# Retention's query-state products of the sample group in 32-column strips, four batches at a time, in two groups

## The chip, the core and the metric

The kernel runs on one core of a Trainium2 chip. Five engines work side by side and meet through semaphores: TensorE (PE in the profile, with its weight loads as PEld), VectorE (DVE), ScalarE (ACT), GpSimd (POOL) and SyncE (SP). The metric is the device time of one execution in microseconds (us), taken as the median of several runs.

## What is computed

One decoder layer for a prompt of 256 tokens and for 8 sample batches of 4 new tokens (32 tokens), 288 tokens in all, with the same weights: a SwiGLU block, then retention and RWKV-7 side by side, a gated merge, and a second SwiGLU block. All numbers are float32. The change touches the sample group's retention, where each batch and head has a state S of 256 x 512 that is read by the queries and then renewed:

```python
def retention_chunk(S, q, k, v, log_g):
    ...
    scores = jnp.einsum('bihd,bjhd->bhij', q, k) * mask[None]
    inner = jnp.einsum('bhij,bjhe->bihe', scores, v)
    ...
    cross = jnp.einsum('bihd,bhde->bihe', q, S) * q_dec[None, :, :, None]
    ...
    S_new = (jnp.exp(log_g * C)[None, :, None, None] * S
             + jnp.einsum('bjhd,bjhe->bhde', k * k_dec[None, :, :, None], v))
    return S_new, inner + cross
```

## The kernel before

**Stages.** The first SwiGLU block and the projections of the first head run first. Then come four units, one for each retention head (RH = 4); a unit is one head of retention and two pairs of RWKV heads (`rw0`, `rw1`). After them the output products and the second SwiGLU block run.

**The weave.** Between the dependent steps of a unit TensorE works on products that depend on nothing in the unit: units 0 to 2 carry the projections of the next head (18 weight blocks), unit 3 the gates (32 blocks). A block is cut into 8 pieces; a piece is two weight tiles by three products (L463 to L465), six matmuls. `GAPS` is a list of named places in the unit, each with a weight, and `parts` deals the 144 pieces (256 in unit 3) over them in proportion. Every engine walks the same list with `weave(name)`: TensorE computes the pieces there; VectorE makes half of a block's low part (L1192) at every fourth piece, and waits there for ScalarE's high part (L874), which ScalarE makes at every eighth, as soon as TensorE has finished the block before; at the last piece of a block ScalarE or VectorE reads a result out of PSUM (VectorE with the rotation L1353 to L1361 at pieces 63 and 79). So a gap's weight sets how long TensorE has other work while VectorE, ScalarE and GpSimd prepare the next step, and also where their shares of the weave stand between their own steps.

**Retention in a unit, in TensorE's order.** Transposes of v and k; scores (L581 to L585); the prompt's new state, two products of 128 x 512 in banks 6 and 7 (L593); the prompt's output (L601, L603, banks 4 and 5); the samples' own part in bank 6 (L612); then for each of the 8 batches two query-state products of 32 rows x 512 columns into partitions 0 to 31 of bank 6 (L620), and two products for the batch's new state (L626) into one of three banks in turn (7, 4, 5). VectorE adds each of these to the state in place (L1427) and counts it in `s_new`; product u waits for update u-3. `q_own` holds a batch's queries and zeros for the other batches, so that the 8 batches sum in one bank. Then ScalarE copies the 32 rows to `o_s` (L1045), TensorE turns them (L548) and the norm follows (L640).

**The states' slots.** `s_ret` has four slots (SLOTS) for eight batches. ScalarE's queue sends the renewed state of a batch to memory (L1041); GpSimd's queue brings batch b+4 into its slot once that has landed (`bring`). In that queue the RWKV rows `last` and the prompt's states `s_out` go out before the second four batches come in.

**VectorE ahead of the updates.** It masks the scores (L1408), makes `k_own` (L1417), then runs `shifts`, about 40 small operations for the RWKV pairs of the same unit (L1377 to L1384), and only then begins with the updates L1427.

## Time and profile before

| | us |
|---|---|
| median of 3 runs (3253.01 to 3257.9) | 3256.34 |
| span of the profiled execution | 3245.0 |
| TensorE busy in it | 3125.5 (96%) |
| VectorE busy | 1537.3 (47%) |
| ScalarE busy | 1110.5 (34%) |
| GpSimd busy | 145.9 (4%) |

The span runs from the first to the last instruction of the profiled execution; the device time of a run holds some 11 us more around it. The units take from about 1015 to 2010 us of the span. A line of the profile's timeline gives start, duration, engine, line and operation of a group of instructions, how many there are, and in brackets how long the engine sat idle before it and for whom. A float32 product of TensorE shows as two matmul records; durations of neighbours overlap, so the step from one start to the next tells the cost.

### The profile page before, as it was taken

The page shows a single profiled execution, that of the slowest core. Times are in us where ns is not written, and L with a number is a line of the kernel's source. Part 1 is how long each engine was busy: PE and PEld are TensorE (multiplying, and loading weights), DVE is VectorE, ACT ScalarE, POOL GpSimd, SP SyncE. Part 2 cuts the span into 40 slices and gives each one's busy share as a digit, 9 for nine tenths or more (in the row PEclk, how much of TensorE's full clock was granted, in tenths as well). Part 3 has the DMA queues.
Part 4 walks back from the last instruction along what each step waited for, and adds up shares of the span by engine and source line. Part 5 has one row for each costly group of instructions (what it writes and reads, how often), then busy time and mean ns, then how long its engine had stood idle before and what let it go on. Part 6 is the DMA issues. An engine that isn't in the chain of part 4 may idle for free.

```text
span 3245.0 us, 54421 instructions
## 1 busy us (share of the span) xinstructions
PE 3125.5 (96%) x22896; PEld 2964.5 (91%) x22896; DVE 1537.3 (47%) x1771; ACT 1110.5 (34%) x1062; POOL 145.9 (4%) x179
## 2 busy tenths in 40 slices
PE   7999999999999999999999999999989999999998
PEld 6999999999898787688688799899989999999997
DVE  5443444444545554553644545445554444444444
ACT  4333333333333333332333334333333333333332
POOL 0000000000000111112011010100000000000000
PEclk9999999999999999999999999999999999999999
DMA  4444454444454423422422544365434444544443
GB/s 168 162 168 153 164 175 168 164 158 156 160 214 145 150 99 106 163 86 89 181 76 95 206 136 148 117 212 185 169 130 168 162 154 165 179 160 165 160 157 140
DMA packets 84285, 495.75 MB, mean 153 GB/s; under 512 B 10032, under 2 KB 10400, under 8 KB 42672
## 3 DMA queue, kind: packets, MB, share of 16 engines
q1 hardware_dynamic: 70704, 444.37, 40.1%
q0 software_dynamic: 8832, 32.57, 2.9%
q10 hardware_dynamic: 4608, 16.78, 1.3%
q8 instruction: 108, 1.77, 0.2%
q14 instruction: 33, 0.27, 0.0%
HBM read 462.88 MB, written 30.80 MB: 152 GB/s over the span
## 4 chain that ended last, share of the span: by engine, by line
PE 83%; DVE 7%; issue 5%; ACT 2%; DMA 2%; POOL 1%; DVEq 0%; SPq 0%; ACTq 0%; POOLq 0%
PE psum L463 25%; PE psum L464 24%; PE psum L465 24%; DVE sb_w_lo L1200 2%; ACT sb_w_hi L874 1%; PE psum L620 1%; PE psum L718 1%; PE psum L742 1%; PE psum L741 1%; DMA sb_s_ret<-in_s_ret 1%; DVE sb_prod L1211 1%; DVE sb_w_lo L1192 1%; DVE sb_h_lo L1221 0%; POOL sb_lm L1725 0%; DMA out_ret_s<-sb_s_ret 0%
## 5 line engine op out<-in xcount | busy, mean ns | idle before, releaser
L463 PE MATMUL psum<-sb_h_hi,sb_w_hi 128*128 128x288 f32 x4528 | 1380.5, 305 | 26.7 <-DVE sb_h_lo L1221 17.5
L465 PE MATMUL psum<-sb_h_hi,sb_w_lo 128*128 128x288 f32 x4528 | 1345.7, 297 | 0.0
L464 PE MATMUL psum<-sb_h_lo,sb_w_hi 128*128 128x288 f32 x4528 | 1345.7, 297 | 0.0
L874 ACT ACTIVATE sb_w_hi<-sb_raw 128x2048 fp32r<-128x2048 f32 (+1 forms) x451 | 793.5, 1759 | 1354.0 <-PE psum L465 1323.7
L1200 DVE TENSOR_TENSOR sb_w_lo<-sb_raw,sb_w_hi 128x2048 fp32r<-128x2048 f32 (+1 forms) x348 | 710.6, 2042 | 880.6 <-ACT sb_w_hi L874 877.9
L463 PEld LDWEIGHTS psum<-sb_h_hi,sb_w_hi 128*128 128x128 f32 x4528 | 858.9, 190 | 56.4 <-issue 41.8
L464 PEld LDWEIGHTS psum<-sb_h_lo,sb_w_hi 128*128 128x128 f32 x4528 | 859.8, 190 | 3.8 <-issue 1.0
L465 PEld LDWEIGHTS psum<-sb_h_hi,sb_w_lo 128*128 128x128 f32 x4528 | 859.4, 190 | 0.4
L463 PE MATMUL psum<-sb_g_hi,sb_w_hi 128*128 128x288 f32 x1408 | 415.4, 295 | 1.5 <-DVE sb_w_lo L1200 0.5
L464 PE MATMUL psum<-sb_g_lo,sb_w_hi 128*128 128x288 f32 x1408 | 416.7, 296 | 0.0
L465 PE MATMUL psum<-sb_g_hi,sb_w_lo 128*128 128x288 f32 x1408 | 414.8, 295 | 0.0
L1192 DVE TENSOR_TENSOR sb_w_lo<-sb_raw,sb_w_hi 128x1024 fp32r<-128x1024 f32 x206 | 250.5, 1227 | 215.0 <-ACT sb_w_hi L874 211.7
L463 PEld LDWEIGHTS psum<-sb_g_hi,sb_w_hi 128*128 128x128 f32 x1408 | 264.7, 188 | 5.4 <-DVE sb_w_lo L1200 5.2
L465 PEld LDWEIGHTS psum<-sb_g_hi,sb_w_lo 128*128 128x128 f32 x1408 | 264.6, 188 | 0.0
L464 PEld LDWEIGHTS psum<-sb_g_lo,sb_w_hi 128*128 128x128 f32 x1408 | 264.6, 188 | 0.0
L1725 POOL TENSOR_TENSOR sb_lm<-sb_mt,sb_levels_m 128x512 f32<-128x512 f32 x48 | 67.2, 1399 | 471.3 <-DVE sb_pt L1497 303.3
L1255 DVE TENSOR_TENSOR sb_prod<-psum,sb_gate 128x576 f32<-128x576 f32 x44 | 33.3, 758 | 103.7 <-PE psum L465 103.7
L463 PE MATMUL psum<-sb_or_hi,sb_w_hi 128*128 128x288 f32 x256 | 76.9, 300 | 5.7 <-DVE sb_or_lo L1612 5.7
L464 PE MATMUL psum<-sb_or_lo,sb_w_hi 128*128 128x288 f32 x256 | 76.7, 300 | 0.0
L465 PE MATMUL psum<-sb_or_hi,sb_w_lo 128*128 128x288 f32 x256 | 76.2, 298 | 0.0
L464 PE MATMUL psum<-sb_m_lo,sb_w_hi 128*128 128x288 f32 x256 | 75.8, 296 | 0.0
L465 PE MATMUL psum<-sb_m_hi,sb_w_lo 128*128 128x288 f32 x256 | 75.5, 295 | 0.0
(314 smaller groups left out, 2468.6 us busy)
## 6 DMA issues: line engine op xcount, KB each, us to landing
sb_raw<-in_gu SPq DMA_DIRECT2D x176, 1024.0 KB, 4.8
sb_raw<-in_down SPq DMA_DIRECT2D x128, 704.0 KB, 4.0
sb_raw<-in_w_mix SPq DMA_DIRECT2D x72, 1024.0 KB, 4.9
sb_raw<-in_w_gates SPq DMA_DIRECT2D x32, 1024.0 KB, 5.2
sb_s_ret<-in_s_ret POOLq DMA_DIRECT2D x32, 512.0 KB, 7.0
out_ret_s<-sb_s_ret ACTq DMA_DIRECT2D x32, 512.0 KB, 3.2
sb_raw<-in_w_ro SPq DMA_DIRECT2D x16, 1024.0 KB, 4.9
sb_raw<-in_w_out SPq DMA_DIRECT2D x16, 1024.0 KB, 4.9
```

Source lines behind the costliest of these rows:

```text
L463: pe.matmul(out, wh, xh, start=start, stop=False)
L464: pe.matmul(out, wh, xl, start=False, stop=False)
L465: return pe.matmul(out, wl, xh, start=False, stop=stop)
L620: mm = pe.matmul(psum[0:NS, 6, :], q_own[:, e, bb, :], s_ret[:, slot, e, :], start=False, stop=(bb == SB - 1 and e == 1))
L718: mm = pe.matmul(psum[:, 5, t * P:(t + 1) * P], lm[:, t, :], xm[:, t, :], start=True, stop=True)
L741: pe.matmul(psum[:, 6, t * 64:(t + 1) * 64], xt[:, t, :], y1, start=True, stop=True)
L742: mm = pe.matmul(psum[:, 7, t * 64:(t + 1) * 64], ym[:, t, :], x2, start=True, stop=True)
L874: act.activation(w_hi[:, slot, 0:cols], raw[:, slot, 0:cols], ACT.Copy).then_inc(hi_made, 1)
L1192: ins = dve.tensor_tensor(w_lo[:, slot, c], raw[:, slot, c], w_hi[:, slot, c].bitcast(F32), ALU.subtract)
L1200: dve.tensor_tensor(w_lo[:, slot, 0:cols], raw[:, slot, 0:cols], w_hi[:, slot, 0:cols].bitcast(F32), ALU.subtract).then_inc(lo_made, 1)
L1255: dve.tensor_tensor(prod[:, :, :], psum[:, s:s + 2, 0:T], gate[:, :, :], ALU.mult).then_inc(hidden, 1)
L1725: pool.tensor_tensor(lm[:, :, :], mt[:, :, :], levels_m[:, n, :].unsqueeze(1).broadcast_to([P, 4, P]), ALU.mult).then_inc(rw_pool, 1)
```

## The change

The query-state products of four batches run as one group, each batch in its own strip of 32 columns of the array, which writes its own 32 partitions of bank 6 (batches 0 to 3 before the prompt's output, 4 to 7 after it). ScalarE now copies 128 rows to `o_s`, and the four strips are summed while they are turned: four products with `fold`, a 128 x 32 matrix of four unit matrices, take the place of four transposes of 32 rows. The first half of the prompt's new state (`kv0`), then the first group and its four state updates, come ahead of the prompt's output; the second half (`kv1`) and the second group follow it. Before the prompt's output TensorE waits until VectorE has made all eight updates of the first group. On GpSimd's queue the second four loads come before `last` and the second half of `s_out`. `fold` is one more constant to load.

The list of gaps changes with it. Retention's weights sum to 28.5 where they were 20.5, RWKV's stay at 91.5, and the pieces are dealt anew:

| pieces in units 0 to 2 | before | after |
|---|---|---|
| v_turned, k_turned, scores | 3, 1, 2 | 2, 2, 2 |
| kv0 | - | 5 |
| kv_s0, kv_s1, kv_s2, kv_s3 | -, -, -, 5 | 1, 1, 1, 2 |
| o_prompt | 2 | 2 |
| kv1 | 2 | 5 |
| kv_s4, kv_s5, kv_s6 | -, 3, - | 1, 1, 1 |
| o_sample, o_sample_turned, norm | 2, 2, 4 | 2, 3, 3 |
| RWKV, rw0 and rw1 | 59 + 59 | 55 + 55 |

From the prompt's state product to the norm's product there are 16 pieces before and 25 after (29 and 43 of unit 3's 256).

```diff
-RET_GAPS = (("v_turned", 2), ("k_turned", 1.5), ("scores", 1.5), ("kv1", 1.5), ("o_prompt", 1.5), ("kv_s3", 4),
...
+RET_GAPS = (("v_turned", 2), ("k_turned", 1.5), ("scores", 1.5), ("kv0", 4), ("kv_s0", 1), ("kv_s1", 1), ("kv_s2", 1),
...
+                def kv(e):
                     for tt in range(2):
-                        mm = pe.matmul(psum[:, 6 + e, :], k_tok[:, tt, e * P:(e + 1) * P], v_tok[:, tt, :],
+                        mm = pe.matmul(psum[:, 7, :], k_tok[:, tt, e * P:(e + 1) * P], v_tok[:, tt, :],
                                        start=(tt == 0), stop=(tt == 1))
                     step(mm)
-                weave("ret_kv1")
-
+
+                def sample(half):
+
+                    for slot in range(SLOTS):
+                        pe.wait_ge(s_landed[slot], h * (16 * SB // SLOTS) + 16 * (half + 1))
+                    for e in range(2):
+                        for j in range(SLOTS):
+                            pe.matmul(psum[j * NS:(j + 1) * NS, 6, :], q_own[:, e, SLOTS * half + j, :], s_ret[:, j, e, :],
+                                      start=(half == 0 and e == 0), stop=(half == 1 and e == 1), skip_group_check=True)
+                    if half == 0:
+                        after(ret_act, RET_ACT, "state0")
+                        after(ret_dve, RET_DVE, "k_owned")
+                    else:
+                        after(ret_act, RET_ACT, "state1")
+                    for bb in range(SLOTS * half, SLOTS * (half + 1)):
+                        for e in range(2):
+                            u = 2 * bb + e
+                            if u >= 3:
+                                pe.wait_ge(s_new, h * (2 * SB) + (u - 2))
+                            step(pe.matmul(psum[:, (7, 4, 5)[u % 3], :], k_own[:, bb, e * P:(e + 1) * P], v_3[:, :],
+                                           start=True, stop=True))
+                        weave(f"ret_kv_s{bb}" if bb < SB - 1 else "ret_o_sample")
+
+                kv(0)
+                weave("ret_kv0")
                 after(ret_dve, RET_DVE, "masked")
+                sample(0)
+
+                pe.wait_ge(s_new, h * (2 * SB) + 2 * SLOTS)
...
                 weave("ret_o_prompt")
...
+                kv(1)
+                weave("ret_kv1")
...
+                sample(1)
...
-                    mm = transpose(psum[:, 6, m * NS:(m + 1) * NS], o_s[:, m * P:(m + 1) * P], NS)
+                    mm = pe.matmul(psum[:, 6, m * NS:(m + 1) * NS], o_s[:, m * P:(m + 1) * P], fold[:, :], start=True, stop=True)
```

On TensorE, at the samples' part of retention in units 0 to 2, before. `sb_s_ret` are the states, `sb_q_own` the queries, and the L626 rows are the products for the new states:

```order
L620 MATMUL psum<-sb_s_ret,sb_q_own 32x512 x2
L626 MATMUL psum<-sb_v_90,sb_k_own 128x512 x2
L620 MATMUL psum<-sb_s_ret,sb_q_own 32x512 x2
L626 MATMUL psum<-sb_v_90,sb_k_own 128x512
L625 ISA
L626 MATMUL psum<-sb_v_90,sb_k_own 128x512
L620 MATMUL psum<-sb_s_ret,sb_q_own 32x512 x2
```

And after, the same place of the changed kernel (its L607 is L620, its L619 is L626, L466 to L468 are a piece of the weave):

```order
L607 MATMUL psum<-sb_s_ret,sb_q_own 32x512 x8
L558 REGISTER_ALU x2
L619 MATMUL psum<-sb_v_91,sb_k_own 128x512 x2
L466 MATMUL psum<-sb_h_hi,sb_w_hi 128x288
L467 MATMUL psum<-sb_h_lo,sb_w_hi 128x288
L468 MATMUL psum<-sb_h_hi,sb_w_lo 128x288
L466 MATMUL psum<-sb_h_hi,sb_w_hi 128x288
L467 MATMUL psum<-sb_h_lo,sb_w_hi 128x288
L468 MATMUL psum<-sb_h_hi,sb_w_lo 128x288
L619 MATMUL psum<-sb_v_91,sb_k_own 128x512
L618 ISA
L619 MATMUL psum<-sb_v_91,sb_k_own 128x512
```

What stood between the state products as pairs now stands once, as eight products, and a piece of the weave stands between the batches. L618 and L625 prepare the wait of the fourth state product for the first update.

On VectorE, in the first RWKV pair of unit 0, before: `sb_st` is the running state, `sb_um` the chunk's input, each waited for by TensorE, and L1192 a share of the weave.

```order
L1551 TENSOR_TENSOR sb_stt<-psum,sb_st 128x128
L1552 SCALAR_TENSOR_TENSOR sb_st<-sb_stt,sb_decays,sb_blocks_m 128x128
L1560 TENSOR_TENSOR sb_um<-psum,sb_gm 64x128
L1192 TENSOR_TENSOR sb_w_lo<-sb_raw,sb_w_hi 128x1024
L1551 TENSOR_TENSOR sb_stt<-psum,sb_st 128x128
```

And after, from the same L1551 on (now L1579):

```order
L1579 TENSOR_TENSOR sb_stt<-psum,sb_st 128x128
L1580 SCALAR_TENSOR_TENSOR sb_st<-sb_stt,sb_decays,sb_blocks_m 128x128
L1378 SCALAR_TENSOR_TENSOR sb_rot<-psum,sb_trig 128x288 x2
L1382 TENSOR_TENSOR sb_qk<-sb_rot 128x288
L1378 SCALAR_TENSOR_TENSOR sb_rot<-psum,sb_trig 128x288 x2
L1386 TENSOR_TENSOR sb_qk<-sb_rot 128x288
L1217 TENSOR_TENSOR sb_w_lo<-sb_raw,sb_w_hi 128x1024
L1588 TENSOR_TENSOR sb_um<-psum,sb_gm 64x128
```

The rotation of piece 79 (L1353 to L1361 before) and a low part moved from the end of the pair, where the gap `mean` held them, to between the third chunk's state and its input `sb_um`.

## Rows read from the trace of the kernel before

**Rows 1.** The page's head.

```profile
span 3245.0 us, 54421 instructions
```

**Rows 2.** Windows: L593 to L640 in units 0 to 3; length, busy by engine, clock.

```profile
1036.40:1080.88 44.48, 40.39 (x176) 22.71 (x175) 27.94 (x67) 8.42 (x11) 3.76 (x7) 1.00 0.55 202
1287.22:1335.67 48.45, 43.34 (x177) 23.90 (x175) 27.90 (x67) 8.38 (x11) 3.77 (x7) 0.93 0.51 186
1547.10:1592.79 45.69, 40.49 (x177) 22.72 (x175) 27.88 (x67) 8.38 (x11) 3.77 (x7) 1.00 0.53 197
1797.42:1848.58 51.16, 50.95 (x254) 33.13 (x253) 30.67 (x68) 12.27 (x12) 3.77 (x7) 1.00 0.58 213
```

**Rows 3.** Timeline of TensorE in unit 1.

```profile
1287.22 3.59 PE L593 MATMUL psum<-sb_v_tok,sb_k_tok 128*128 128x512 f32 x8
...
1290.25 0.69 PE L463 MATMUL psum<-sb_h_hi,sb_w_hi 128*128 128x288 f32 x1
...
1292.24 0.59 PE L601 MATMUL psum<-sb_scores,sb_v_tok 128*128 128x256 f32 x2
...
1294.77 0.38 PE L463 MATMUL psum<-sb_h_hi,sb_w_hi 128*128 128x288 f32 x1
...
1296.53 1.04 PE L612 MATMUL psum<-sb_v_tok_s,sb_scores 32*32 32x512 f32 x2
1297.50 1.90 PE L620 MATMUL psum<-sb_s_ret,sb_q_own 128*32 128x512 f32 x4
1299.34 0.74 PE L626 MATMUL psum<-sb_v,sb_k_own 96*128 96x512 f32 x2
...
1307.39 0.30 PE L463 MATMUL psum<-sb_h_hi,sb_w_hi 128*128 128x288 f32 x1
...
1313.07 1.90 PE L620 MATMUL psum<-sb_s_ret,sb_q_own 128*32 128x512 f32 x4 [1.53 <-DMA sb_s_ret<-in_s_ret]
...
1318.19 3.62 PE L620 MATMUL psum<-sb_s_ret,sb_q_own 128*32 128x512 f32 x4 [2.56 <-DMA sb_s_ret<-in_s_ret]
...
1333.60 0.40 PE L548 MATMUL psum<-sb_ident,sb_o_s 32*128 32x32 f32 x4 [1.03 <-ACT sb_o_s L1045]
```

**Rows 4.** The same view in unit 0: products in three strips of 32 columns.

```profile
1027.54 1.07 PE L564 MATMUL psum<-sb_ident,sb_vg 128*32 128x128 f32 x24
```

**Rows 5.** Timeline of VectorE in unit 1, from the scores to the updates.

```profile
1285.63 0.42 DVE L1408 TENSOR_TENSOR sb_scores<-psum,sb_rc 128x256 f32<-128x256 f32 x1 [1.46 <-PE psum L585]
...
1290.16 0.16 DVE L1377 COPY sb_zs<-sb_pp 128x8 f32<-128x8 f32 x1
...
1299.63 0.16 DVE L1384 COPY sb_last<-sb_zs 128x8 f32<-128x8 f32 x1
1300.12 1.23 DVE L1192 TENSOR_TENSOR sb_w_lo<-sb_raw,sb_w_hi 128x1024 fp32r<-128x1024 f32 x1 [0.33 <-DVE sb_last L1384]
1301.27 2.72 DVE L1427 SCALAR_TENSOR_TENSOR sb_s_ret<-sb_s_ret,sb_rc,psum 128x512 f32<-128x512 f32 x4
```

**Rows 6.** GpSimd's queue in unit 1: the loads of batches 4 and 7.

```profile
1306.95 0.54 POOL L1684 DMA_DIRECT2D sb_s_ret<-in_s_ret  x1 [4.09 <-DMA out_ret_s<-sb_s_ret]
...
1316.66 0.53 POOL L1684 DMA_DIRECT2D sb_s_ret<-in_s_ret  x1 [4.88 <-DMA out_ret_s<-sb_s_ret]
```

**Rows 7.** The view of tile `sb_s_ret`, 1270 to 1345 us: times to landing.

```profile
DMA to landing us min/median/max: 2.6/5.8/8.2
```

**Rows 8.** Timeline of VectorE in unit 1: the rotation of piece 79.

```profile
1432.40 0.82 DVE L1353 SCALAR_TENSOR_TENSOR sb_rot<-psum,sb_trig 128x288 f32<-128x288 f32 x2 [0.34 <-PE psum L465]
...
1435.31 1.23 DVE L1192 TENSOR_TENSOR sb_w_lo<-sb_raw,sb_w_hi 128x1024 fp32r<-128x1024 f32 x1
```

**Rows 9.** Timeline of ScalarE in unit 1: a block's high part.

```profile
1469.65 1.90 ACT L874 ACTIVATE sb_w_hi<-sb_raw 128x2048 fp32r<-128x2048 f32 x1
```

**Rows 10.** TensorE's waits, 1341 to 1530 us: total us, times, longest.

```profile
PE psum L718 <- POOL sb_lm_s L1730: 1.9, 2, 1.4
...
PE psum L775 <- DVE sb_st L1552: 1.6, 1, 1.6
```

99 lines of the change are left out of this document (49 added, 50 removed).

## Prediction

> **What bounds the kernel now.** I began with the share of busy time, where TensorE has 96%, and then asked where in the units it is not busy, since the change touches the units alone. The windows from the prompt's state product (L593) to the norm's product (L640) are 44.5, 48.5, 45.7 and 51.2 us long in units 0 to 3, and TensorE is busy for all of the last but about 0.2 us, while it lacks 4 to 5 us in each of the first three [rows 2]. The timeline of unit 1 names them: 1.53 and 2.56 us for the fifth and sixth batch's state to come from memory, 1.03 us for the copy of the output [rows 3]. Behind the second of these waits four records of L620 took 3.62 us where they take 1.90: TensorE's clock was at 1.2 instead of 2.4 GHz, and the window's mean is 0.93 [rows 2, 3]. So TensorE's own work is the bound, with waits in between, and a microsecond taken off it counts only if what it waits for next is ready.
>
> **What the strips take away.** A batch's two query-state products last from 1297.50 to 1299.34, 1.84 us [rows 3]; 8 batches are 14.7 us. The trace has no four strips, but three: 24 records of 128 columns in 1.07 us, 45 ns each [rows 4]. A record of 512 columns takes 1.84 / 4 = 0.46 us, a quarter of it would be 0.115, so three strips did the work of 2.6. Four strips then need between 1.84 (all four at once) and 2.1 us (with the loss of those three); one after the other they would need 7.4. I take 1.9 for a group, nearest to the three strips. The work falls by 14.7 - 3.8 = 10.9 us in a unit, 44 us in all.
>
> The Trainium skill (TensorE: Matmul & The Clock Gate, Part 3, Measured speedup vs the span model) gives 2.38 for three column strips of 512 columns; rows show 2.6 for 128 columns. By the skill a group would last 7.4 / (2.38 x 4 / 3) = 2.3 us, as an estimate 0.4 more, and the kernel some 2 us more.
>
> **What is added.** Turning with `fold` reads 128 rows: four products have no row; they lie between the transposes' 0.40 us [rows 3] and eight records of 0.115, 0.92 us; I take 0.9, since each has full weights, +0.5 a unit. ScalarE's copy keeps its 512 columns: nothing. The constant `fold` loads long before it is used: nothing. A piece of the weave takes 0.83 us ((1313.07 - 1.53 - 1307.39) / 5), and five of them behind a state product of the prompt 4.45, as the two there take 1.99 [rows 3].
>
> **The first group, in unit 1, from L593 = 0.** TensorE: half of the prompt's state 1.5, five pieces 4.45, the group 2.05 with the change of shape, the first batch's pair 0.6, a piece 0.8, one product 0.2: at 9.6 it stands before the fourth state product, which needs the first update. VectorE decides: from the scores on it has no gap worth naming, 4.5 us to `shifts`, 9.6 us of `shifts`, then a low part, and begins the updates at 1301.27, which is 14.05; the first ends at 14.8 [rows 5]. Nothing of that order changes. In the kernel before, the prompt's output and its pieces cover that time; now they stand behind it. **So TensorE waits 5.2 us, and the 5.5 us that the first group gains are gone.** The clock will fall behind such a wait, but TensorE then follows VectorE anyway: eight updates at 0.66 ((2.72 - 0.74) / 3), a low part of 1.2, and the prompt's output starts at 20.8.
>
> **The second group.** Behind 20.8: prompt's output 2.55 (1292.24 to 1294.77), two pieces 1.75 (1294.77 to 1296.53), half of the state 1.5 (half of 1287.22 to 1290.25), five pieces 4.45, the samples' own part 1.1 (1296.53 to 1297.50, and the change of shape) [rows 3]: TensorE arrives at 32.2. All four slots must have landed. Before, the last load was issued at 1316.66 and landed some 5.8 us later, at about 35.2 [rows 6, 7]. Now the fourth batch's update ends about 1 us earlier, and `last` and half of `s_out` are no longer ahead in the queue; I take 33, with 32 (no wait) and 37 (landing at the longest, 8.2) as ends. From 32.7: the group 1.9, eight updates with a low part 7.1, ScalarE's copy 0.7, `fold` 0.9, three pieces 2.5: the norm's product stands at about 45.7.
>
> **The sum of the stretch.** It now holds nine pieces more, worth 7.5 us, taken from elsewhere. So it gains 44.5 + 7.5 - 45.7 = 6.3 us in unit 0, 10.2 in unit 1 (whose waits cost the clock too) and 7.5 in unit 2. In unit 3 the same steps with the longer gaps give an arrival of 12.9 at the fourth product, a wait of 2 us, no wait for memory (the gap `kv1` alone has nine pieces), and 53.5: 51.2 + 14 pieces (11.6) - 53.5 = 9.3. Together 33 us.
>
> **What the pieces leave behind.** In units 0 to 2 eight pieces go from RWKV and one from the norm: 7.5 us of cover a unit. There TensorE is already at the edge: it waits for GpSimd before L718 twice, for VectorE at L775 [rows 10]. Where a chain through VectorE and ScalarE sets the time, a lost piece comes back as a wait of 0.83. Moreover the weave's shares stand elsewhere. In `rw0` the rotation (2.9 us from 1432.40) and a low part now come before the third chunk's `sb_um`, which TensorE needs 2.15 us (a piece, L775, a piece) after piece 79: 2.9 + 1.15 + 0.3 - 2.15, a new wait of 2.2 [rows 8]. In `rw1` block 14 now begins inside `prod_s`: VectorE waits there for ScalarE (read-out 0.6, high part 1.9 [rows 9]), makes a low part (1.15), only then `xt` and `xm`, and GpSimd's mask follows: L718's wait grows by about 2.6. In `rw0`, at `y32`, block 9 does the same for about 0.9. On the other side a low part leaves the place before L775, whose 1.6 goes [rows 10]. With 1.0 for the norm and `kk` and 1.0 over the rest this is some 7 us a unit. Its ends: 0, if other work hides it all, and 10, if the clock falls too. I take 7.3: 22 us in three units. Unit 3 has twice the pieces a gap and shows no such waits: 1.5. `v_turned` has a piece less ahead of v's copies: 0.25 a unit. For the clock at 1.2 GHz behind the new waits I take 3, between 0 and 8.
>
> 33 - 22 - 1.5 - 0.75 - 3 = 5.7, so the profiled span of 3245.0 [rows 1] falls by 5 to 6 us. The median 3256.3 stands 11.3 above that span, and I move it by as much: **3251 us**.
>
> **The rivals.** *The cover was to spare* (0.29): the chains in RWKV have slack where I see none, and only a third of the 22 us comes back: 3251 - 14 = 3237, with half of it 3240; I put it at 3240. For it: the small total of waits there. Against: rows of waits at the very places that lose pieces.
>
> *The slowest slot* (0.23): the second group needs four landings where the kernel before needed one at a time. Two waits now fall together, and if the last state lands at 37 instead of 33, TensorE waits 4.3 us in units 0 to 2, and the clock behind it costs 1.7 each time, as at 1318.19. That is 18 us: 3269, slower than now; half of it, landing at 35, gives 3259. The point from which it decides is a landing 2 us after 32.7. For it: landings of up to 8.2 us while weights load beside them. Against: in unit 3 the pieces hide it.
>
> *The strips run one after the other* (0.05): a group lasts 7.4. The first is still hidden by the wait for VectorE, the second is not: 5.5 in four units and 3 in unit 3, 3276. Against it stand 24 records in 1.07 us [rows 4].
>
> *All 44 us arrive* (in the first rival's tail): it would need VectorE's updates 5 us earlier, and nothing in the change moves them. The Trainium skill (TensorEngine Tiling (Array Packing), PSUM Bottleneck) warns that tiling does not speed up what empties PSUM. The updates here are such work: 16 x 0.66 = 10.6 us a unit that did not change.
>
> **How the numbers follow.** The forecast has 0.43, from 3245 to 3258. The range takes in the first rival and the slowest slot: 3237 to 3269. A measurement of this kernel tells about 0.2% (6.5 us) from no change. Faster by more than that: 0.26 of the first rival and 0.11 of the forecast's lower edge, 0.37. Slower: 0.17 of the slowest slot, 0.05 of the strips, 0.03 of the forecast's upper edge, 0.25. The rest, 0.38, is no change.
>
> **What would show it.** Eight products of a group in 1.9 to 2.1 us; a wait of about 5 us for VectorE before the fourth state product in units 0 to 2, 2 in unit 3; a wait of 0 to 4 us for memory before the second group; the stretch at 45.7 and 53.5 us; in RWKV new waits at the third chunk's L781 and before L718 of `rw1`. The forecast is wrong if the updates start earlier than 14 us behind L593, if the RWKV waits grow by less than 4 us a unit, or if the last slot lands behind 35.

## The result

| | before | after |
|---|---|---|
| median | 3257.12 us | 3328.73 us |
| single runs | 3253.01 to 3259.42 | 3324.45 to 3331.2 |
| span of the profiled execution | 3245.0 | 3329.6 |
| TensorE busy in it | 3125.5 | 3140.7 |

The changed kernel is slower: the ratio is 1.0218, with a 95% interval of 1.0203 to 1.0232. The forecast was 3251 us with a range of 3237 to 3269; it missed by 78 us, on the wrong side.

The two spans differ by 84.6 us, the medians by 71.6. In every run for which both are on record the time is some 1.6 us above the span (3331.2 and 3329.6 here), not 11 us, as I had taken it before: the profiled execution of the kernel before was some 10 us faster than its median. So the account below, which goes by the two traces, is some 13 us too large in all, and no row tells in which stretch.

The page of the kernel after, its head, TensorE's busy time and its granted clock in 40 slices (answer to [rows 1]):

```profile
span 3329.6 us, 54468 instructions
...
PE 3140.7 (94%) x22912; PEld 3010.9 (90%) x22912; DVE 1536.1 (46%) x1771; ACT 1109.9 (33%) x1061; POOL 147.3 (4%) x180
...
PEclk9999999999999979889889999989999999999999
```

The strips take some 41 us off TensorE's work (eight groups of 1.9 us that take 7.05 in one strip), and yet its busy time is 15 us longer: the clock row has an 8 or a 7 in six slices, where the kernel before has only nines. The idle time grew from 119.5 to 188.9 us.

The windows of the kernel after, from the prompt's first state product (now L597) to the norm's product (now L655) in units 0 to 3; columns as in [rows 2]: length, busy by engine, granted clock:

```profile
1038.54:1098.19 59.65, 43.97 (x235) 34.77 (x234) 31.33 (x69) 11.66 (x12) 3.75 (x7) 0.80 0.50 175
1313.20:1370.97 57.77, 43.05 (x234) 33.52 (x233) 30.73 (x69) 11.06 (x12) 3.76 (x7) 0.82 0.49 175
1586.40:1644.42 58.02, 44.59 (x234) 35.31 (x233) 31.32 (x69) 11.68 (x12) 3.76 (x7) 0.79 0.51 186
1860.58:1926.97 66.39, 54.38 (x342) 46.33 (x341) 36.91 (x74) 16.61 (x15) 3.76 (x7) 0.90 0.56 200
```

And from the norm's product to the next unit, first in the kernel before, then in the kernel after:

```profile
1080.88:1287.22 206.34, 193.10 (x1480) 174.19 (x1479) 102.10 (x179) 74.91 (x105) 31.27 (x33) 0.97 0.30 102
1335.67:1547.10 211.43, 199.10 (x1480) 179.26 (x1480) 102.23 (x179) 74.96 (x105) 31.28 (x33) 0.94 0.29 100
1592.79:1797.42 204.63, 196.97 (x1509) 178.53 (x1509) 104.01 (x182) 76.93 (x106) 31.27 (x33) 0.97 0.30 105
```

```profile
1098.19:1313.20 215.01, 197.25 (x1425) 176.87 (x1425) 97.73 (x176) 71.91 (x103) 30.64 (x33) 0.91 0.26 91
1370.97:1586.40 215.43, 196.94 (x1427) 176.85 (x1426) 98.41 (x177) 72.51 (x104) 30.58 (x33) 0.91 0.27 91
1644.42:1860.58 216.16, 199.51 (x1457) 179.40 (x1456) 98.14 (x177) 73.82 (x104) 30.61 (x33) 0.92 0.27 93
```

This is the account of the 84.6 us of span. The four stretches are longer by 15.2, 9.3, 12.3 and 15.2 us, 52.0 together; 34.0 of that are the pieces moved into them (nine in units 0 to 2, 14 in unit 3, 0.83 each), so **18 us are lost in the stretch** where 33 were forecast as a gain. TensorE was idle in the four stretches for 55.8 us instead of 14.6; the strips should have given back some 39 of these 41 us (`fold` counted), and the other 16 are longer busy time at a granted clock of 0.79 to 0.90 (an estimate: what is left over). The windows behind hold nine pieces fewer and are still 8.7, 4.0 and 11.5 us longer: with the 22.4 us of pieces that left, **47 us are lost in units 0 to 2 behind the norm's product**, nearly all of which is RWKV. Behind the stretch of unit 3 it is 6.2 and 11.6, 18 us. The last 2 us lie ahead of the units.

The timeline of TensorE in unit 1 after the change (answers [rows 3]):

```profile
1318.98 1.92 PE L607 MATMUL psum<-sb_s_ret,sb_q_own 128*32 128x512 f32 x16
...
1328.05 0.79 PE L619 MATMUL psum<-sb_v,sb_k_own 96*128 96x512 f32 x1 [5.45 <-DVE sb_s_ret L1451]
...
1335.02 0.59 PE L632 MATMUL psum<-sb_scores,sb_v_tok 128*128 128x256 f32 x2
...
1345.01 1.04 PE L643 MATMUL psum<-sb_v_tok_s,sb_scores 32*32 32x512 f32 x2
1351.82 3.64 PE L607 MATMUL psum<-sb_s_ret,sb_q_own 128*32 128x512 f32 x16 [5.77 <-DMA sb_s_ret<-in_s_ret]
...
1364.13 0.62 PE L619 MATMUL psum<-sb_v,sb_k_own 96*128 96x512 f32 x1 [3.50 <-DVE sb_s_ret L1451]
```

The first group takes 1.9 us, as forecast; the wait for VectorE behind it is 5.45. The second group starts 38.6 us behind L597, not 32.7, although TensorE stands before it at 32.9, nearly as forecast. It then runs at 1.2 GHz (3.64 us), and a wait of 3.50 us follows that I had not seen. ScalarE's and VectorE's timelines explain that one:

```profile
1357.86 2.27 ACTq L1054 DMA_DIRECT2D out_ret_s<-sb_s_ret  x2
1360.25 1.91 ACT L889 ACTIVATE sb_w_hi<-sb_raw 128x2048 fp32r<-128x2048 f32 x1 [18.51 <-DVE sb_s_ret L1451]
```

```profile
1362.20 1.23 DVE L1217 TENSOR_TENSOR sb_w_lo<-sb_raw,sb_w_hi 128x1024 fp32r<-128x1024 f32 x1 [2.63 <-ACT sb_w_hi L889]
1363.34 2.71 DVE L1451 SCALAR_TENSOR_TENSOR sb_s_ret<-sb_s_ret,sb_rc,psum 128x512 f32<-128x512 f32 x4
```

A weight block begins (piece 24) among the updates. ScalarE's high part for it stands behind the store of batch 5, which waits for VectorE's update; VectorE's low part waits for the high part (2.63 us), and the next update stands behind the low part. Two queues, each in order, wait for one another in turns.

### The profile page after: what moved, and what is told of

The parts are those of the page before. It is cut to its first block, busy times and chain, and to the rows that moved or that the text cites. A ratio compares the mean times of both kernels' runs of the same rounds, so it can differ in the third digit from the quotient of the medians.

```text
span 3329.6 us, 54468 instructions
## 1 busy us (share of the span) xinstructions
PE 3140.7 (94%) x22912; PEld 3010.9 (90%) x22912; DVE 1536.1 (46%) x1771; ACT 1109.9 (33%) x1061; POOL 147.3 (4%) x180
## 4 chain that ended last, share of the span: by engine, by line
PE 79%; DVE 8%; issue 6%; ACT 3%; DMA 2%; POOL 1%; DVEq 0%; ACTq 0%; SPq 0%; POOLq 0%
PE psum L466 24%; PE psum L467 23%; PE psum L468 23%; ACT sb_w_hi L889 2%; DVE sb_w_lo L1225 2%; PE psum L733 1%; DVE sb_w_lo L1217 1%; PE psum L757 1%; PE psum L756 1%; DMA out_ret_s<-sb_s_ret 1%; DMA sb_s_ret<-in_s_ret 1%; DVE sb_prod L1236 1%; POOL sb_lm L1756 1%; DVE sb_s_ret L1451 1%; DVE sb_h_lo L1246 0%
## 5 line engine op out<-in xcount | busy, mean ns | idle before, releaser
L466 PE MATMUL psum<-sb_h_hi,sb_w_hi 128*128 128x288 f32 x4528 | 1393.8, 308 | 38.5 <-DVE sb_h_lo L1246 19.1
L468 PE MATMUL psum<-sb_h_hi,sb_w_lo 128*128 128x288 f32 x4528 | 1357.6, 300 | 0.0
L466 PEld LDWEIGHTS psum<-sb_h_hi,sb_w_hi 128*128 128x128 f32 x4528 | 870.8, 192 | 69.6 <-issue 51.7
L467 PEld LDWEIGHTS psum<-sb_h_lo,sb_w_hi 128*128 128x128 f32 x4528 | 871.4, 192 | 6.2 <-issue 1.9
L468 PEld LDWEIGHTS psum<-sb_h_hi,sb_w_lo 128*128 128x128 f32 x4528 | 871.1, 192 | 0.4
L466 PE MATMUL psum<-sb_g_hi,sb_w_hi 128*128 128x288 f32 x1408 | 415.9, 295 | 1.4 <-DVE sb_w_lo L1225 0.5
L468 PE MATMUL psum<-sb_g_hi,sb_w_lo 128*128 128x288 f32 x1408 | 414.6, 294 | 0.0
L466 PEld LDWEIGHTS psum<-sb_g_hi,sb_w_hi 128*128 128x128 f32 x1408 | 264.7, 188 | 5.3 <-DVE sb_w_lo L1225 5.2
L468 PEld LDWEIGHTS psum<-sb_g_hi,sb_w_lo 128*128 128x128 f32 x1408 | 264.6, 188 | 0.0
L466 PE MATMUL psum<-sb_or_hi,sb_w_hi 128*128 128x288 f32 x256 | 77.0, 301 | 5.7 <-DVE sb_or_lo L1640 5.7
L468 PE MATMUL psum<-sb_or_hi,sb_w_lo 128*128 128x288 f32 x256 | 76.3, 298 | 0.0
L466 PE MATMUL psum<-sb_m_hi,sb_w_hi 128*128 128x288 f32 x256 | 75.9, 296 | 0.2 <-issue 0.2
```

Of the source, the lines that this page charges most:

```text
L466: pe.matmul(out, wh, xh, start=start, stop=False)
L467: pe.matmul(out, wh, xl, start=False, stop=False)
L468: return pe.matmul(out, wl, xh, start=False, stop=stop)
```

## The experiments

Lengths are in us: the stretch in units 0 to 3, then the windows behind units 0 to 2. How far they vary by themselves can be read from the kernels that share one list from the norm on. With that of the kernel before (before, strips_alone, cover_back, cover_shifts, cover_shifts_pairs, queue_order, queue_last, queue_last_serial) the three windows behind sum to 622.4 to 633.4 us, with that of the kernel after (after, order_alone, shares_alone, no_first_stores, after_queue, shifts_later) to 636.9 to 646.6. By the two averages the loss there is 37 us and not 47.

| run | median | ratio to before (95%) | stretch | behind |
|---|---|---|---|---|
| before | 3257.1 | | 44.5, 48.5, 45.7, 51.2 | 206.3, 211.4, 204.6 |
| after | 3328.7 | 1.0218 (1.0203-1.0232) | 59.7, 57.8, 58.0, 66.4 | 215.0, 215.4, 216.2 |
| strips_alone | 3276.0 | 1.0059 (1.0042-1.0075) | 50.5, 52.7, 52.9, 55.4 | 210.5, 209.9, 209.0 |
| order_alone | 3339.4 | 1.0261 (1.0238-1.0284) | 61.8, 59.4, 61.4, 74.9 | 209.2, 214.3, 214.5 |
| shares_alone | 3297.5 | 1.0144 (1.0107-1.0181) | 48.3, 49.4, 48.5, 73.0 | 207.2, 214.3, 215.5 |
| cover_back | 3264.3 | 1.0028 (1.0016-1.0039) | 47.9, 48.3, 46.2, 59.9 | 209.5, 207.2, 209.6 |
| cover_half | 3254.6 | 1.0010 (1.0000-1.0020) | 48.4, 48.9, 48.3, 56.2 | 201.0, 204.3, 203.4 |
| one_place | 3303.3 | 1.0150 (1.0127-1.0172) | 55.9, 59.6, 55.5, 66.6 | 210.1, 207.0, 212.6 |
| two_places | 3298.5 | 1.0133 (1.0117-1.0150) | 58.5, 55.9, 60.0, 66.7 | 206.7, 206.5, 208.6 |
| filled | 3323.3 | 1.0229 (1.0205-1.0253) | 60.3, 56.8, 57.0, 66.6 | 213.2, 216.4, 215.4 |
| no_first_stores | 3295.8 | 1.0128 (1.0108-1.0147) | 49.9, 50.8, 51.4, 63.5 | 215.4, 211.1, 216.2 |
| after_queue | 3307.1 | 1.0157 (1.0140-1.0174) | 55.7, 57.7, 54.9, 63.9 | 215.2, 214.0, 216.2 |
| shifts_later | 3305.7 | 1.0160 (1.0131-1.0190) | 57.3, 49.5, 47.9, 65.9 | 209.4, 212.0, 216.5 |
| cover_shifts | 3253.2 | 0.9999 (0.9985-1.0013) | 45.4, 40.8, 41.7, 58.3 | 209.6, 208.3, 205.6 |
| cover_shifts_pairs | 3254.9 | 1.0004 (0.9991-1.0017) | 48.0, 41.5, 40.9, 62.3 | 209.9, 206.3, 208.7 |
| queue_order | 3232.7 | 0.9928 (0.9912-0.9945) | 45.1, 37.9, 37.9, 48.3 | 211.8, 211.5, 210.2 |
| queue_last | 3221.2 | 0.9905 (0.9888-0.9922) | 37.2, 38.2, 37.2, 45.4 | 208.6, 207.6, 206.9 |
| queue_last_serial | 3259.7 | 1.0013 (1.0002-1.0024) | 47.5, 46.6, 46.7, 55.6 | 210.2, 209.5, 208.7 |
| queue_less | 3231.9 | 0.9933 (0.9914-0.9952) | 38.4, 39.7, 39.7, 42.1 | 206.8, 211.9, 212.3 |
| **queue_half** | **3208.7** | **0.9859 (0.9843-0.9876)** | 37.9, 36.0, 36.9, 51.9 | 203.5, 203.1, 208.4 |

### The three parts of the change, one at a time

**Strips alone.** The edit is made in the kernel before; its order and its gaps stay, `fold` and the copy of 128 rows come along:

```diff
                 for bb in range(SB):
-                    slot = bb % SLOTS
-                    pe.wait_ge(s_landed[slot], h * (16 * SB // SLOTS) + 16 * (bb // SLOTS + 1))
-                    for e in range(2):
-                        mm = pe.matmul(psum[0:NS, 6, :], q_own[:, e, bb, :], s_ret[:, slot, e, :], ...)
+                    if bb % SLOTS == 0:
+                        for slot in range(SLOTS):
+                            pe.wait_ge(s_landed[slot], h * (16 * SB // SLOTS) + 16 * (bb // SLOTS + 1))
+                        for e in range(2):
+                            for j in range(SLOTS):
+                                pe.matmul(psum[j * NS:(j + 1) * NS, 6, :], q_own[:, e, bb + j, :], s_ret[:, j, e, :], ...)
```

> The kernel before in its own order and with its own shares of the weave; only the query-state products run in strips, four batches at a time, with the copy of 128 rows and the turning with fold. Theory (the strips free TensorE where VectorE and the memory set the pace, so they bring next to nothing): a group takes 1.9 us instead of 7.4, TensorE waits some 2 us before the fourth state product, whose update VectorE starts only 14 us behind the prompt's first state product, and some 10 us for the fourth slot of the second group; the stretch from the first state product to the norm's product stays within 2 us of 44.5, 48.5, 45.7 us in units 0 to 2 and falls by 3 to 8 us in unit 3; what lies outside the stretch is unchanged; time 3240 to 3265. Rival (the strips pay, the new order spoils them): the stretch falls by 8 to 11 us in each unit, 3215 to 3225.

It came out at 3276, above the theory's range and far from the rival's. TensorE's timeline in unit 1:

```profile
1308.61 1.92 PE L624 MATMUL psum<-sb_s_ret,sb_q_own 128*32 128x512 f32 x16
1313.15 0.50 PE L631 MATMUL psum<-sb_v,sb_k_own 96*128 96x512 f32 x1 [1.72 <-DVE sb_s_ret L1432]
...
1330.60 3.64 PE L624 MATMUL psum<-sb_s_ret,sb_q_own 128*32 128x512 f32 x16 [7.97 <-DMA sb_s_ret<-in_s_ret]
```

Both waits are there, 1.72 and 7.97 us where some 2 and 10 were expected. What I left out is the clock: the group behind the long wait takes 3.64 us in all four units, and the stretches' mean clock is 0.75 to 0.91, where the kernel before has 0.93 to 1.00. So in the order of the kernel before, all that the strips free turns into waits for VectorE and the memory and into the lower clock, and 20 us more are lost.

**The order alone.** The changed kernel, with the eight products of a group one after another in rows 0 to 31 and turned by transposes:

```diff
-                            pe.matmul(psum[j * NS:(j + 1) * NS, 6, :], q_own[:, e, SLOTS * half + j, :], s_ret[:, j, e, :],
+                            pe.matmul(psum[0:NS, 6, :], q_own[:, e, SLOTS * half + j, :], s_ret[:, j, e, :],
```

> The changed kernel's order and shares of the weave, but the query-state products one after another in one strip of 32 rows, 7.4 us for a group, turned by transposes as before. Theory: in units 0 to 2 the first group's 5.5 us more fill the wait before the fourth state product (5.4 us down to 0), the second group's 5.5 us come on top of the landing of its last slot, so the stretch grows by some 4 to 6 us in each of units 0 to 2 and by 2 to 8 in unit 3, less what the clock gives back; 3340 to 3355. Rival (the strips gave nothing in this order, all is waits): within 5 us of 3329.

3339.4, just below the range: the strips are worth 11 us in this order, not 44. The wait for VectorE behind the first group was 0.27 us in unit 1, its place taken by the group's 7.05 us.

```profile
1314.03 7.05 PE L606 MATMUL psum<-sb_s_ret,sb_q_own 128*32 128x512 f32 x16
...
1323.06 0.50 PE L619 MATMUL psum<-sb_v,sb_k_own 96*128 96x512 f32 x1 [0.27 <-DVE sb_s_ret L1451]
```

**The weave's shares alone.** The kernel before, with this list (and VectorE's `shifts` ahead of its gap kv1; with these shares, as I read the program, its queue and TensorE's would otherwise wait for each other in unit 3):

```diff
-RET_GAPS = (("v_turned", 2), ("k_turned", 1.5), ("scores", 1.5), ("kv1", 1.5), ("o_prompt", 1.5), ("kv_s3", 4),
-            ("kv_s5", 2), ...
+RET_GAPS = (("v_turned", 2), ("k_turned", 1.5), ("scores", 1.5), ("kv1", 4.5), ("o_prompt", 3.5), ("kv_s3", 6),
+            ("kv_s5", 3), ...
```

> The kernel before, with neither strips nor the new order; only its shares of the weave are changed, so that every gap from the samples' output copy on has the very pieces of the changed kernel (34 of 144 pieces before RWKV in units 0 to 2, not 26; 61 of 256 in unit 3, not 47), and VectorE does the shifts ahead of its part of the gap kv1 and not behind it. Theory (lost cover in RWKV is the largest part of the loss, and it needs nothing else of the change): the windows from the norm's product to the next unit grow to 214 to 217 us although they hold 8 pieces (6.6 us) less, the stretch grows by about its 9 more pieces (7.5 us) or less, since some fill waits; time 3295 to 3320. Rival (the pieces are only moved, and the loss needs the strips' waits): 3250 to 3275.

3297.5: 42 us are lost without any strip. The windows behind units 1 and 2 are 214.3 and 215.5, the changed kernel's; the one behind unit 0, at 207.2, is not. At equal pieces the three windows behind lose 37 us (14.5 and 22.4 of pieces), what follows unit 3's stretch 10, unit 3's stretch another 10 (21.8 less 11.6 of pieces), and the stretches of units 0 to 2, whose pieces fill waits, gain 15. In unit 3 `shifts` was moved too, so its 10 us may not be the shares' alone.

**The changed kernel with the cover given back.** Only the list of gaps is changed, so that every gap from the norm on holds the pieces that it held before:

```diff
-            ("kv0", 4), ("kv_s0", 1), ("kv_s1", 1), ("kv_s2", 1), ("kv_s3", 1), ("o_prompt", 2), ("kv1", 4), ("kv_s4", 1), ...
+            ("kv0", 1.5), ("kv_s0", .5), ("kv_s1", .5), ("kv_s2", .5), ("kv_s3", 1), ("o_prompt", 1.5), ("kv1", 2.5), ("kv_s4", .5), ...
```

> The changed kernel with smaller shares of the weave in the retention's stretch (sum 20.5 as before the change, not 28.5), so that every gap from the norm's product on has the very pieces of the kernel before. Theory (most of the loss is lost cover and the lower clock in RWKV): the windows from the norm's product to the next unit return from 215, 215 and 216 us to 206, 211 and 205 within 2 us, and the tail behind unit 3 too; the stretch keeps waits of 7 to 8 us before the fourth state product and 6 to 9 us for memory and lasts 54 to 57 us in units 0 to 2; time 3280 to 3300. Rival (the loss is in the stretch alone, and fewer pieces there only lengthen its waits): the stretch does not shorten by more than 3 us, and the time stays within 10 us of 3329.

3264.3, even less than expected. **So 64 of the 72 us hang on this list of numbers alone**; strips and new order together cost 7 to 10. By the windows, at equal pieces, 43 of them lie behind the stretch in units 0 to 2, 17 behind that of unit 3, and only 6 in the four stretches.

### Is it the number of pieces, or their places?

I took the loss to grow with each piece that RWKV gives up, and tried the list half way between (sum 24.5).

> The changed kernel with shares of the retention's stretch half way between its own (sum 28.5, 3329 us) and those of the run with the cover given back (sum 20.5, 3264 us): sum 24.5. Theory (each piece that RWKV loses comes back as a wait and a lower clock): about half way, 3288 to 3305. Rival (a few pieces at certain waits do it, the rest is spare): under 3280 or over 3315.

**3254.6: this theory fell.** Five pieces a unit (seven in unit 3) were taken from what follows the stretch, and next to nothing was lost (a ratio of 1.0010 to the kernel before); the windows behind the norm are 201 to 204 us, 14 us shorter in sum than before the change with 12 us fewer pieces in them. The next 4 of weight cost 74 us. So the number of pieces alone does not set the loss; where the ones that remain stand is the other thing that the list changes. The waits of TensorE at the place that had grown most, total us, times, longest, in the kernel after, then in the half-way one:

```profile
PE psum L733 <- POOL sb_lm_s L1761: 21.3, 7, 3.9
```

```profile
PE psum L733 <- POOL sb_lm_s L1761: 7.8, 7, 1.7
```

What stands ahead of that wait in unit 1, `rw1`, of the kernel after, on ScalarE, VectorE, GpSimd and TensorE:

```profile
1507.67 0.65 ACT L988 ACTIVATE sb_vg<-psum 128x576 f32<-128x576 f32 x1 [5.79 <-PE psum L468]
1508.22 1.90 ACT L889 ACTIVATE sb_w_hi<-sb_raw 128x2048 fp32r<-128x2048 f32 x1
```

```profile
1510.16 1.23 DVE L1217 TENSOR_TENSOR sb_w_lo<-sb_raw,sb_w_hi 128x1024 fp32r<-128x1024 f32 x1 [2.84 <-ACT sb_w_hi L889]
1511.30 0.68 DVE L1541 TENSOR_TENSOR sb_xt<-sb_lm,sb_ident 128x512 f32<-128x512 f32 x1
...
1512.13 0.40 DVE L1548 TENSOR_TENSOR sb_xm<-sb_xm,psum 128x256 f32<-128x256 f32 x1
```

```profile
1512.62 2.18 POOL L1756 TENSOR_TENSOR sb_lm<-sb_mt,sb_levels_m 128x512 f32<-128x512 f32 x1 [4.91 <-DVE sb_xm L1548]
1514.76 0.31 POOL L1761 TENSOR_TENSOR sb_lm_s<-sb_ms,sb_levels_m 32x64 f32<-32x64 f32 x1
```

```profile
1515.19 2.07 PE L733 MATMUL psum<-sb_xm,sb_lm 128*128 128x128 f32 x8 [3.92 <-POOL sb_lm_s L1761]
```

Piece 112 begins a block. It is the last of the gap `prod_s`, so the read-out, the high part and the low part (3.8 us in a row) come ahead of `xt` and `xm`, and GpSimd's masks wait for those. With the half-way list piece 112 is the first of the next gap, `x1`. The test is to move that piece alone, in the changed kernel:

```diff
+PLACES = {"rw1_prod_s": 2.7, "rw1_x1": 2.5}
 GAPS = tuple(("ret_" + n, w) for n, w in RET_GAPS) + tuple(
-    (f"rw{q}_" + n, w) for q in range(2) for n, w in RW_GAPS)
+    (f"rw{q}_" + n, PLACES.get(f"rw{q}_" + n, w)) for q in range(2) for n, w in RW_GAPS)
```

> The changed kernel; in the second pair of each unit one piece of the weave (two in unit 3) moves from the gap behind the samples' products to the gap behind the first inverse products, so that piece 112, which begins a block and brings a high part of 1.9 us and a low part of 1.2, stands behind the level's masks and not ahead of them. No gap's neighbours lose cover: the same pieces stand ahead of the wait at L733. Theory (the loss in RWKV hangs on a few places where a block begins between VectorE's products and GpSimd's mask): the wait of 3.9 us there falls to under 1.5 in units 0 to 2, with some of the clock behind it, 3310 to 3321. Rival (the number of pieces taken from RWKV does it): within 5 us of 3329.

**3303.3: one piece, moved over one product, gave 25 us back.** The same wait of the same unit, and the sums of that wait in this run and in the next:

```profile
1505.41 1.15 PE L735 MATMUL psum<-sb_xm,sb_lm 128*128 128x128 f32 x8 [0.71 <-POOL sb_lm_s L1763]
```

```profile
PE psum L735 <- POOL sb_lm_s L1763: 9.9, 6, 2.6
```

The wait fell by 3.2 us a unit, the three windows by 5.0, 8.4 and 3.5, and the time by more than both. The clock makes part of the rest, as the product behind the wait shows, at 2.07 us with it and 1.15 without; another 6.7 us of the profiled difference lie behind the stretch of unit 3, and 4 in the stretches, which the edit does not touch. The windows' sum of 629.7 us is below all six of the old list (636.9 to 646.6), so the gain is clear, its exact size less so. The time is 7 us below the range. Moving pieces 56 and 57 in `rw0` as well (`"rw0_prod_s": 2.0, "rw0_x1": 3.2`):

> As the run before in this call, and in the first pair of a unit two pieces more (three in unit 3) move in the same way, so that piece 56 stands behind the masks too; its wait at L733 is 2.6 us. Theory: that wait falls to about 1, and the time by 3 to 8 us against that run. Rival: the two pieces are missed ahead of the products before, and nothing is gained.

```profile
PE psum L735 <- POOL sb_lm_s L1763: 2.1, 3, 0.7
```

3298.5, and the waits at L733 are all but gone. The step of 5 us is within the spread of the single runs (3293 to 3300 against 3297 to 3311), but the windows' sum falls again, to 621.8. So 30 of the 74 us between the two lists are shown to be places. 44 us remain to the half-way list: 24 in the stretch at equal pieces, as the windows show, and the rest in parts that I did not take apart; there number and place are not told apart.

**Does the clock do it, or the wait?** Idle work ahead of L733, into columns 384 to 511 of bank 7 that nobody reads:

```diff
                 for s in LEVELS:
+                    if s == 2 and not isinstance(p, int):
+                        for _ in range((19, 32)[q]):
+                            pe.matmul(psum[:, 7, 384:512], ident[:, :], ident[:, :], start=True, stop=True, ...)
                     after(rw_pool, RW_POOL, f"lm{s}" if s > 2 else "lm_s2")
```

> The changed kernel; before the second level's products of RWKV (the row that waits for GpSimd's mask, 2.6 us in the first pair of a unit and 3.9 in the second), TensorE in units 0 to 2 runs 19 and 32 products of 128 x 128 into unused columns of PSUM, some 2 and 3.4 us of work whose result nobody reads. It changes no wait's end, only whether TensorE is idle before it. Theory (half of the loss in RWKV is the clock at 1.2 GHz behind such waits): the half-clock stretches behind these two rows go, the windows from the norm's product to the next unit shrink by 3 to 6 us each, 3312 to 3322. Rival (the clock falls for the other, smaller waits all the same, or the loss is the waits alone): windows within 2 us of 215 to 216, time within 6 us of 3329.

The run is not clean. I had counted a product as one record; the trace has two for each:

```profile
1510.22 7.31 PE L732 MATMUL psum<-sb_ident 128*128 128x128 f32 x64
1517.36 1.06 PE L736 MATMUL psum<-sb_xm,sb_lm 128*128 128x128 f32 x8
```

The fill outlasts the wait, by 3 us here (10.0 us from L722 to L736, where the kernel after has 6.9). The windows still have their old length, within 2 us, and their mean clock is 0.94 instead of 0.91. So the higher clock paid for a fill that was some 3 to 5 us a unit too long. That is an estimate of what the clock costs there, not a proof. The time, 3323, is within 6 us of the kernel after, as the rival had it, but with a fill of the wrong length that does not decide between the two.

A cleaner row lies in unit 3, which this edit leaves alone. From the norm's product to the first output product, in the kernel after and in this run:

```profile
1926.97:2191.33 264.36, 249.97 (x1862) 232.57 (x1863) 121.64 (x182) 100.42 (x121) 26.83 (x24) 0.96 0.36 120
```

```profile
1923.87:2180.95 257.08, 242.40 (x1863) 225.88 (x1863) 121.61 (x182) 100.40 (x121) 26.82 (x24) 0.99 0.37 123
```

The same instructions, the same idle time (14.4 and 14.7 us), and 7.3 us between them, all of it TensorE's busy time at another mean clock. `no_first_stores` and `after_queue`, whose code is the same there, have the short form (257.1), `shifts_later` the long one (264.4). So the clock alone moves such a window by 7 us. The kernel after is at the long end, and 7 of the 18 us behind its unit 3 are this, not the list.

### The stretch: the memory, the shifts and ScalarE's queue

**The wait for memory.** The stores of batches 0 to 3 are left out (that part of the output is missing), and a load waits for the update alone:

> The changed kernel without the stores of the new state of batches 0 to 3 (that part of the output is left out); the load of batch b + 4 waits for the update of batch b alone. It prices the wait for memory before the second group. Theory (the chain update, store, load of the last slot is what ends late): the last load is issued some 9 us earlier, the wait of 4.5 to 6.9 us in units 0 to 2 and the half-clock group behind it (1.7 us each) go, 3300 to 3315. Rival (the transfers are limited by the rate of the memory, weights among them, not by the store's latency): the wait stays at over 2 us, 3318 to 3329.

3295.8, 33 us less; the wait before the second group is gone in all three units (6.94, 5.77 and 4.47 us before), the group is back at 1.92 us, and the last load of unit 1 is issued 21.8 us behind L597 instead of 30.9. That is more than the 22 us that waits and slow groups had. The store's landing ahead of the load is thus what the second group waits for; but with the stores their traffic goes as well, and this run does not tell that from their place in the chain.

Why the chain was longer than forecast is argued, not shown. Between 10 and 40 us behind L597 the kernel after issues loads of two blocks of 1 MB, the kernel before and the half-way list one. In unit 1 its second group starts at 38.6 us, that of the half-way list at 33.7, and with the cover given back at 34.4. No run moves the weights' loads alone. GpSimd's queue in unit 1 of the kernel after, the loads of batches 4 and 7 (answers [rows 6]):

```profile
1333.40 0.53 POOL L1712 DMA_DIRECT2D sb_s_ret<-in_s_ret  x1 [16.34 <-DMA out_ret_s<-sb_s_ret]
...
1344.13 0.53 POOL L1712 DMA_DIRECT2D sb_s_ret<-in_s_ret  x1 [1.94 <-DMA out_ret_s<-sb_s_ret]
```

The last load is issued 30.9 us behind L597 (29.4 before), and TensorE starts 7.7 us later.

**ScalarE's queue.** In the changed kernel ScalarE does its part of a gap first and issues the store behind it:

```diff
                 for bb in range(SLOTS):
-                    send(bb)
                     weave(f"ret_kv_s{bb}")
+                    send(bb)
```

> The changed kernel; only ScalarE's queue is reordered: around the updates of the samples' state it does its part of the weave first and issues the store of a batch (which waits for that batch's update) behind it. Theory (a high part queued behind a store that waits for an update comes late, VectorE's low part waits for it, and the next updates behind the low part): the wait of some 3.5 us among the second group's state products goes in units 0 to 2; the waits before the fourth state product (5.4 us) and for memory stay; 3312 to 3322. Rival (VectorE's own low parts and updates are what TensorE waits for there): within 5 us of 3329.

3307.1: 22 us for two lines exchanged (and the same two for the second group), 5 us beyond the range. The wait of 3.50 us in unit 1 fell to 2.03 and did not go. Of the 17.6 us between the two profiled executions 9.6 lie in the stretches and 7.3 behind that of unit 3, where it is the clock described above; so the reordering itself is worth more like 15 us than 22 (an estimate).

**VectorE's shifts.** They go behind the first group's updates (unit 3 keeps them; so does unit 0, whose body VectorE runs ahead of its loop, which I had not meant):

```diff
-                shifts(h)
+                if isinstance(h, int):
+                    shifts(h)
                 weave("ret_kv0")
 ...
                 for bb in range(SLOTS):
                     state_s(bb)
+                if not isinstance(h, int):
+                    shifts(h)
```

> The changed kernel, with VectorE's shifts behind the updates of batches 0 to 3 in units 0 to 2 (in unit 3 they stay). Theory: the wait of 5.4 us before the fourth state product falls to 1 us or less, the stores start 5 us earlier, and with them the last slot lands 4 to 5 us earlier; the copy of the prompt's output waits for the shifts (ScalarE's queue), up to 26 us behind the first state product, which is still before the landing at 33; the stretch falls from 58 to 60 us to 53 to 55, time 3305 to 3318. Rival (the transfers' rate and VectorE's own order set the second group, so that the wait only moves): the wait before the second group grows by the 5 us, time within 8 us of 3329.

3305.7. The stretches of units 1 and 2 fall by 8.2 and 10.1 us, that of unit 0, which the edit did not reach, by 2.3.

**Together, with the cover given back:**

> The changed kernel with the smaller shares of the retention's stretch (as in the run with the kernel before's cover, 3264 us) and, in units 0 to 2, VectorE's shifts behind the first group's four updates and the low part of the gap behind the prompt's output. Theory: of the wait of 6.7 us before the fourth state product some 5 us go in each of three units, the last slot lands 3 to 5 us earlier, and the second group starts that much earlier; 3246 to 3256, the kernel before's time. Rival (the shifts, now between the groups, end only 25 us behind the first state product, and ScalarE's copy of the output behind them; the second group waits as before): 3260 to 3270.

3253.2, the kernel before's time, with only two units reached. The variant with the second group in two pairs of strips:

> As the run before it in this call, but the second group's products in two pairs of batches, two strips each (1.85 us a pair, 3.7 us instead of 1.9 for the four), so that the first pair needs two landings and not four. Theory (the slowest slot): the first pair starts 1 to 3 us earlier, which pays the 1.8 us, and in unit 3, which has no wait for memory, it costs 1.8 us; within 5 us of the run before it. Rival (the fourth slot's landing is what the second group waits for longest): 4 to 9 us faster than that run.

3254.9: no difference, so four landings at once are not the trouble once the stores start early.

**ScalarE's order in that kernel**, and its copy of the samples' output right behind the second group (`kv_s4e`) instead of behind the last store:

> The kernel with the smaller shares and the later shifts (3253 us), with ScalarE's queue reordered as in the run before in this call, and its copy of the samples' output taken as soon as the second group's products are done, not behind the last store. Theory: the waits of 3.5 us in the first group's updates and of 2.1 us before the turning with fold go in units 0 to 2, those of 2.9 and 5.0 us in unit 3; 3230 to 3243, faster than the kernel before by 0.4 to 0.8%. Rival (each wait comes back behind it, since VectorE's shifts end at the same time): within 5 us of 3253.

3232.7, 0.7% faster than the kernel before. **And the shifts moved in all four units**, unit 3 with its pieces taken out of the first group (`RET_LAST`, 15 of them behind the second half of the prompt's state):

> As the run before in this call, and in unit 3 too the shifts stand behind the first group's updates, for which that unit's pieces are moved from the first group to the gap behind the second half of the prompt's state (15 pieces there). Theory: the wait of 5.3 us in unit 3 goes and 2 to 3 us come back where pieces are missing among the updates; 2 to 4 us faster than that run. Rival (unit 3 is set by the pieces' own low parts): no change within 1.5 us.

3221.2, 11.5 us less, where 2 to 4 were expected: most of the rest is unit 0 (45.1 to 37.2), which this edit reaches as well. **What the strips are worth here:**

> As the run before in this call, with the query-state products one after another in one strip, turned by transposes. It shows what the strips are worth once the waits around them are gone. Theory (the strips pay where TensorE is the bound, and the second group is partly covered by the shifts): 22 to 36 us slower than that run. Rival (the strips' time goes into waits in any order): less than 10 us slower. All of the strips' 10.9 us a unit would be 42 us.

**38.5 us, of 42 possible**, and above the range of 22 to 36. It is the same edit as in `order_alone`, where it was worth 11. Less in the stretch than 20.5:

> The fastest kernel so far (3221 us) with yet smaller shares in the retention's stretch, sum 18 instead of 20.5, so that RWKV gets 2 to 3 pieces a unit more than in the kernel before. Theory: RWKV's waits for GpSimd and VectorE shrink by 1 to 3 us a unit, but the stretch, whose second group now has fewer pieces ahead of its landing, waits as much longer, and a high part falls among the second group's updates; within 6 us of 3221. Rival (cover in RWKV is worth more than anywhere else): 3205 to 3214.

3231.9, 11 us slower, outside the theory. The waits for GpSimd's mask are 13.2 us in sum where `queue_last` has 5.8, which points to the places again; no run moved them in this kernel. And the half-way list, whose places had been harmless:

> The fastest kernel so far (3221 us: shifts behind the first group's updates in all units, ScalarE's high parts ahead of its stores) with the shares of the run half way (sum 24.5), in unit 3 with its additional pieces in the gap behind the second half of the prompt's state. Theory (those shares have their blocks at harmless places, and the windows from the norm's product to the next unit were 201 to 204 us with them, not 207 to 209): 3205 to 3218. Rival (the stretch, which holds four more pieces, has no wait left for them): 3219 to 3230.

**3208.7 us, 1.4% faster than the kernel before.** Its stretch in units 0 and 1, with 21 pieces where that of [rows 2] has 16:

```profile
1037.85:1075.74 37.89, 34.69 (x211) 26.40 (x210) 27.52 (x66) 9.14 (x11) 3.75 (x7) 0.95 0.68 240
1279.27:1315.28 36.01, 33.27 (x210) 25.63 (x209) 27.43 (x66) 8.93 (x11) 3.76 (x7) 1.00 0.69 254
```

## The prediction, step by step

The sum was 33 - 22 - 1.5 - 0.75 - 3 = 5.7 us of gain. By the traces the 33 of the stretch were a loss of 18; the waits in RWKV took 19.7 where 22 were forecast; and beside them stood 27 us of longer busy time where I had 3 for the clock; unit 3's tail took 18 and not 1.5. So three steps failed: the landing of the last slot with what follows it, unit 3, and above all the price of the lower clock.

- **The strips' own time: right.** 1.9 us forecast, 1.86 to 1.92 measured at the full clock, against 7.05 for the same eight products in one strip. The Trainium skill (TensorE: Matmul & The Clock Gate, Part 3, Measured speedup vs the span model) had led to an estimate of 2.3 us; the measurement decides.
- **The first group: right in units 0 to 2.** Wait 5.2, measured 5.45; the prompt's output at 20.8, measured 21.8; arrival at the second group at 32.2, measured 32.9.
- **The first group in unit 3: wrong.** Forecast was a wait of 2 us. The gap kv0 has eight pieces there and crosses into a new block, whose low part VectorE does behind `shifts`; TensorE waited 9.12 us inside the pieces. I had counted pieces as time and not asked what each needs.
- **The landing: wrong.** I took 33 with 37 as the longest; it was 38.6. I assumed that the last load is issued earlier than before, while it was issued 1.5 us later, and TensorE started 7.7 us behind it where I had 5.8. That figure of [rows 7] was misread: it is the median of loads and stores together, while on the page of the kernel before the loads of the states alone have a median of 7.0 us. Nor did I add up what the moved pieces put on the same memory. The rival *slowest slot* had the mechanism, with its price too small.
- **Behind the landing: 13.0 us forecast, 19.2 measured** in unit 1. The clock cost 1.7 us in the group alone; the 3.50 us of the two queues was not in the sum, though all its parts could be read from the order of the two engines.
- **The waits in RWKV: right in size, wrong as a price.** Forecast 22 us in three units; the idle time there grew by 19.7. Some luck is in that: the terms listed for a unit add up to 6.1 us, not to the 7.3 that I took. The chain before L718, now L733, in `rw1`, block 14 inside `prod_s`, came as described, +3.4 us in unit 1 against the 2.6 forecast, and the wait before L775 went. But the windows lost 47 us. I had 3 us for the clock, within 0 to 8; its mean fell from 0.94-0.97 to 0.91-0.92. The other 27 us are busy time: TensorE worked 593.7 us in the three windows where the kernel before worked 589.2 with 22.4 us of pieces more. By the mean clocks it spent 112 us of them at 1.2 GHz and not 50, and 62 us more at half speed cost 31 at most (an estimate, with 1.2 and 2.4 GHz as the two levels). So most of the 27 fits the clock, as the row of unit 3 shows it alone; the exact share stays open.
- **What a lost piece costs: the rule was wrong.** I priced each at 0.83 where a chain sets the time. The half-way list shows next to 0 for the first five, `one_place` 25 us in all for a single one a unit (two in unit 3) at the wrong place.
- **Unit 3's tail: wrong.** 1.5 us forecast, 18 lost. I reasoned that twice the pieces cover everything. TensorE's idle time up to the first output product grew from 7.8 to 14.4 us; 7 us more are the clock, as shown above; the remaining 4 stay open.
- **The rivals.** *All 44 us arrive* failed for the reason given, VectorE; the remedy turned out to be in the program (`shifts` later), and then 38.5 of 42 came. *One after another* is refuted. *Cover to spare* was true of the first half of what was taken and false of the second. None of the rivals reached 3329, since each was one mechanism and here three came together.
